# Two layers on one core: the order of the first loads and turns changed, and two orders of operations at the starts of two down projections

## The reference

```
h  = rmsnorm(x, norm_pre[0])                  # per position, over 2048 channels
z, xbc, dt = split(h @ ssd_w_in)              # 8 groups: 64 heads of 64, state of 128
xs, B, C = split(silu(causal_dwconv(xbc, 4 taps)))
dt = softplus(dt + dt_bias); a = dt * -exp(a_log)
y  = (C B^T * decay) (xs dt) + states from the chunk before + xs * d_skip
x  = x + rmsnorm(rmsnorm(y * silu(z)) @ ssd_w_out)
h  = rmsnorm(x);  q = h @ xa_w_q;  k, v = rmsnorm(mem) @ xa_w_kv      # 4 heads of 128
x  = x + rmsnorm(softmax(q k^T / sqrt(128)) v @ xa_w_o)
x  = x + rmsnorm(conv_ffn(rmsnorm(x)))        # 2048 -> 2 x 5632 -> 2048
# second layer: sparse and forgetting attention, then another conv_ffn, then the final norm
```

## Time and profile before

| | |
|---|---|
| median of three runs | 2713.67 us (2711.70 to 2715.04) |
| the profiled execution | 2714.08 us, of which the span is 2712.5 us |
| PE busy | 2678.1 us, 99% of the span |
| DVE, ACT, POOL busy | 64%, 49%, 6% |
| DMA | 503.41 MB, mean 186 GB/s |
| chain that ended last | PE 95%, DVE 2%, ACT 1%, issue 1% |

### The profile page before, as it was taken

The page is one execution under the profiler, slowest core; times in us unless marked ns, Lnnn a source line. Parts: engine busy times, 40 slices in busy tenths (PEclk is TensorE's granted clock), DMA queues, the critical chain, the costliest instruction groups (busy, mean ns, idle before and its releaser), DMA issues.

```text
span 2712.5 us, 37724 instructions
## 1 busy us (share of the span) xinstructions
PE 2678.1 (99%) x13921; PEld 2278.6 (84%) x13921; DVE 1736.5 (64%) x2133; ACT 1337.3 (49%) x1659; POOL 155.2 (6%) x130
## 2 busy tenths in 40 slices
PE   7999999999999999999999999999999999999998
PEld 6888888888778888888888887888888888888887
DVE  6777777754666767666744475644576766676444
ACT  5555555533566554555544464443465455545433
POOL 2311111100000000000000010000000000000000
PEclk9999999999999999999999999999999999999999
DMA  7555555565453555555555565434555555555552
GB/s 236 179 179 187 184 171 187 199 244 190 155 200 126 205 197 186 186 190 193 195 200 197 186 215 187 140 128 164 189 186 190 186 199 187 197 186 204 199 187 107
DMA packets 223163, 503.41 MB, mean 186 GB/s; under 512 B 15374, under 2 KB 50474, under 8 KB 202992
## 3 DMA queue, kind: packets, MB, share of 16 engines
q1 hardware_dynamic: 218160, 476.81, 52.2%
q0 software_dynamic: 4464, 24.99, 2.6%
q10 hardware_dynamic: 464, 0.59, 0.1%
HBM read 498.07 MB, written 4.28 MB: 185 GB/s over the span
## 4 chain that ended last, share of the span: by engine, by line
PE 95%; DVE 2%; issue 1%; ACT 1%; DMA 0%; SPq 0%; DVEq 0%; POOLq 0%; POOL 0%; ACTq 0%
PE PB L1214 14%; PE T L1214 13%; PE T L1522 12%; PE PB L1522 11%; PE PB L1168 9%; PE PB L1170 9%; PE PB L1169 9%; PE T L1525 6%; PE PB L1525 6%; PE T L1400 1%; PE T L1324 1%; DVE hT L1781 1%; DVE w_lo L1752 1%; PE T L1456 0%; DMA x<-in_x_dram 0%
## 5 line engine op out<-in xcount | busy, mean ns | idle before, releaser
L1752 DVE TENSOR_TENSOR w_lo<-raw,w_hi 128x2048 fp32r<-128x2048 f32 (+3 forms) x468 | 1037.6, 2224 | 598.4 <-ACT w_hi L714 596.5
L714 ACT ACTIVATE w_hi<-raw 128x2048 fp32r<-128x2048 f32 (+3 forms) x468 | 868.8, 1859 | 894.4 <-PE T L1214 384.6
L1168 PE MATMUL PB<-w_hi,hT 128*128 128x512 f32 (+3 forms) x1280 | 485.3, 379 | 5.4 <-DVE hT L1781 3.4
L1522 PE MATMUL T<-hT,w_hi 128*128 128x512 f32 x1408 | 489.7, 391 | 0.0
L1170 PE MATMUL PB<-w_hi,hT 128*128 128x512 f32 (+3 forms) x1280 | 471.3, 368 | 0.0
L1169 PE MATMUL PB<-w_lo,hT 128*128 128x512 f32 (+3 forms) x1280 | 471.1, 368 | 0.0
L1522 PE MATMUL PB<-hT,w_hi 128*128 128x512 f32 x1280 | 444.6, 391 | 0.0
L1525 PE MATMUL T<-hT,w_lo 128*128 128x256 f32 x1408 | 394.3, 280 | 0.0
L1525 PE MATMUL PB<-hT,w_lo 128*128 128x256 f32 x1280 | 358.4, 280 | 0.0
L1522 PEld LDWEIGHTS T<-hT,w_hi 128*128 128x128 f32 x1408 | 263.4, 187 | 58.0
L1214 PE MATMUL PB<-w_hi,hT 128*128 128x512 f32 x1120 | 305.2, 392 | 6.6 <-issue 3.0
(11 more groups left out here) (286 smaller groups left out, 2036.8 us busy)
## 6 DMA issues: line engine op xcount, KB each, us to landing
raw<-in_ffn_w_up_dram SPq DMA_DIRECT2D x88, 1024.0 KB, 5.1
raw<-in_w_up_dram SPq DMA_DIRECT2D x88, 1024.0 KB, 5.0
raw<-in_ssd_w_in_dram SPq DMA_DIRECT2D x64, 1024.0 KB, 5.2
raw<-in_ffn_w_down_dram SPq DMA_DIRECT2D x44, 1024.0 KB, 4.8
raw<-in_w_down_dram SPq DMA_DIRECT2D x44, 1024.0 KB, 4.8
raw<-in_w_in_dram SPq DMA_DIRECT2D x40, 1024.0 KB, 5.1
raw<-in_ssd_w_out_dram SPq DMA_DIRECT2D x32, 1024.0 KB, 4.8
raw<-in_ssd_w_in_dram SPq DMA_DIRECT2D x64, 256.0 KB, 3.2
```

The costliest lines, as they stand in the source:

```text
L714: nc.scalar.activation(dst, src, ACT.Copy).then_inc(hi_ready, 1)
L1168: nc.tensor.matmul(o, h, wh[:, c, :], start=(j == first and c == 0), stop=False)
L1522: ins = nc.tensor.matmul(banks[f][:, :], wh[:, c, s], both, start=(k == 0), stop=False)
L1752: V.tensor_tensor(dst, src, h.bitcast(F32), ALU.subtract).then_inc(lo_ready, 1)
```

## The change

It has three parts.

**Entry.** SP issues quad j of BCD ahead of block j of x (L549, then L555 in the changed file). ACT and DVE split quad j before they work on block j. PE turns block 0 before the first product, and block j + 1 inside quad j, after the first of its four chunks. Only the first 64 rows of parameters (`FIRST_ROWS`: the gains of three norms and of `norm_mem`) are loaded at once, by ACT's queue; POOL waits for block 2 of x before it issues the three broadcasts and the other 1008 rows, and PE turns those rows after quad 0 of unit 1 rather than before it. DVE copies them out two quads later than before. PE gets 14 small matmuls on the identity (`warm`), 4 before the first rows, 6 behind them, 4 behind block 0. ACT gets one tiny copy of 128x1 before its loop. The softplus scratch moves, since the rows lie longer in their place.

**`wout`.** In the last group, ACT and DVE make `down_first` right behind quad 0 of `wout` rather than after the convolution of xs, and DVE multiplies in the decays (L1977, `decayed`) behind quad 3 rather than before it.

**`xo`.** ACT splits chunks 0 and 1 before the high part of quad 3 rather than after; DVE copies out all four heads and splits chunks 0 and 1 before the low part of quad 3.

```diff
 NROWT = -(-NCOL // P)
+FIRST_ROWS = 4 * KC
...
-T_PLAN = [("params0", (0, 0, 1, 0)), (N_X, (2,) * 4), ("params", (1, 1, 0, 0)),
+T_PLAN = [("params0", (0, 0, 1, 0)), (N_X, (2,) * 4), ("params", (1, 1, 1, 0)),
...
         acsT = misc[0:HEADS, :]
-        sp_tmp = [big[:, 4096 + 128 * k:4096 + 128 * (k + 1)] for k in range(8)]
+        sp_tmp = [big[:, 5376 + 128 * k:5376 + 128 * (k + 1)] for k in range(8)]
...
             for name, a0, r, k in ROW_LOADS:
-                if (r < P) == first_tile:
+                if (r < FIRST_ROWS) == first_tile:
...
             for j in range(4):
+                load_bcd(j)
...
                     sp.dma_start(xt[:, tt, at], I["x"][0, tt * P:(tt + 1) * P, at]).then_inc(x_landed[j], 16)
-                load_bcd(j)
...
+            pool.wait_ge(x_landed[2], 32)
...
-            def down_first(name, ready):
+            def down_first(name, ready, js=range(4)):
...
                 act.wait_ge(quad_used, 4 * unit - 3)
-                for j in range(4):
+                for j in js:
...
             load_rows(act, True)
-            act.wait_ge(cols_ready, 1)
+            act.wait_ge(pool_own, 2)
+            nc.scalar.activation(mx[:, 0:1], ones[:, 0:1], ACT.Copy)
             for j in range(4):
+                hi_bcd(j)
+                if j == 0:
+                    act.wait_ge(cols_ready, 1)
...
                     h_hi(N_X, tt, "norm_pre", 0, None, (j,))
-                hi_bcd(j)
...
                 hi_next(0)
+                if not nxt:
+                    down_first("wout", lambda j: act.wait_ge(te[3], tb[3] + 2))
...
                 nc.scalar.activation(big[:, 9216:10240], big[:, 9216:10240], ACT.Silu).then_inc(xc_ready, 1)
-                if not nxt:
-                    down_first("wout", lambda j: act.wait_ge(te[3], tb[3] + 2))
...
                 prob_out(h)
-            hi_unit(U_XO, js=(3,))
-            down_first("xo", lambda h: xa_taken(act, h, (4, 4, 2, 2)[h]))
+            for js in ((0, 1), (2, 3)):
+                down_first("xo", lambda h: xa_taken(act, h, (4, 4, 2, 2)[h]), js)
+                if js == (0, 1):
+                    hi_unit(U_XO, js=(3,))
...
-            def up(q, pair, n, evac_before, after=None, norm=None):
+            def up(q, pair, n, evac_before, after=None, norm=None, inside={}):
...
                         if c in between:
-                            norm_transposes(norm[0], norm[1], 1, (between[c],))
+                            between[c]()
...
                         products(j, (0,), FIRST_TILE_ORDER[0], FIRST_TILE_ORDER[3],
-                                 {1: 0, 2: 1} if j == FIRST_TILE_ORDER[3] else {})
+                                 {1 + b: lambda b=b: norm_transposes(norm[0], norm[1], 1, (b,)) for b in range(2)}
+                                 if j == FIRST_TILE_ORDER[3] else {})
...
                         pe.wait_ge(lo_ready, q + j + 1)
-                    ins = products(j, (1,) if by_tile else (0, 1))
+                    ins = products(j, (1,) if by_tile else (0, 1), between=inside.get(j, {}))
...
-            pe.wait_ge(rows0_landed, 16 * sum(r < P for _, _, r, _ in ROW_LOADS))
-            turn_rows(0, 2, 0).then_inc(tf[2], 1)
...
+            def warm(n):
...
+                for _ in range(n):
+                    nc.tensor.matmul(T[3][:, 0:P], ident[:, :], ident[:, :], start=True, stop=True)
...
+            warm(4)
+            pe.wait_ge(rows0_landed, 16 * sum(r < FIRST_ROWS for _, _, r, _ in ROW_LOADS))
+            nc.tensor.transpose(T[2][:, 0:FIRST_ROWS], rows[0:FIRST_ROWS, 0, :], ident[0:FIRST_ROWS, 0:FIRST_ROWS]).then_inc(tf[2], 1)
+            warm(6)
             def turn_other_rows():
-                pe.wait_ge(rows_landed, 16 * sum(r >= P for _, _, r, _ in ROW_LOADS))
+                pe.wait_ge(rows_landed, 16 * sum(r >= FIRST_ROWS for _, _, r, _ in ROW_LOADS))
+                bank_free(2, TB["params"][2])
+                turn_rows(0, 2, 0).then_inc(tf[2], 1)
...
                     turn_group(N_X, 0)
-                    turn_group(N_X, 1)
-                    up(q, pair[0], BCD, None, {0: lambda: turn_group(N_X, 2), 1: lambda: turn_group(N_X, 3), 3: turn_other_rows}, (N_X, None))
+                    warm(4)
+                    up(q, pair[0], BCD, None, None, (N_X, None), {j: {0: lambda b=j + 1: turn_group(N_X, b)} for j in range(3)})
                 up(q + 4, pair[1], BLK, g * 3 + (E_SSD - 1) if prev else None,
-                   {2: lambda: (cumulative_sums(), turn_bc(g))} if not prev else
+                   {0: turn_other_rows, 2: lambda: (cumulative_sums(), turn_bc(g))} if not prev else
...
             dve.wait_ge(tf[2], 1)
-            V.tensor_copy(cols[:, 0:P], T[2][:, 0:P]).then_inc(te[2], 1)
+            V.tensor_copy(cols[:, 0:FIRST_ROWS], T[2][:, 0:FIRST_ROWS]).then_inc(te[2], 1)
...
             for j in range(4):
+                lo_unit(U_SSD, BCD, (j,))
...
                     h_lo(N_X, tt, "norm_pre", 0, (j,))
-                lo_unit(U_SSD, BCD, (j,))
             def other_cols():
+                dve.wait_ge(tf[2], TB["params"][2] + 1)
+                V.tensor_copy(cols[:, FIRST_ROWS:P], T[2][:, FIRST_ROWS:P]).then_inc(te[2], 1)
...
                             means(N_X, D)
-                            other_cols()
...
                             time_steps()
+                        if j == 2:
+                            other_cols()
...
                 lo_next(0)
+                if not nxt:
+                    down_first("wout")
...
                 lo_next(2)
-                if not nxt:
-                    down_first("wout")
-                decayed(g)
-                lo_next(3)
+                if nxt:
+                    decayed(g)
+                    lo_next(3)
+                else:
+                    lo_next(3)
+                    decayed(g)
...
                 lo_unit(U_XO, js=(1 + k,))
-            lo_unit(U_XO, js=(3,))
...
             xa_out(3)
+            lo_unit(U_XO, js=(3,))
```

## The result

The changed kernel takes 2706.49 us (median of 8 runs, 2705.59 to 2707.99) against 2714.24 us (8 runs) for the kernel before beside it: 7.8 us less, a ratio of 0.9972 (95% interval 0.9963 to 0.9981). Predicted were 2705.9 us and 7.8 us less. The profiled execution took 2706.38 us, its span went from 2712.5 to 2704.7. The total is right, but not every term: the entry gave 2.4 for 1.7, `wout` 1.2 for 1.45, `xo` 4.6 for 4.6, and 0.35 was lost between them.

The account below looks back on a forecast made before the run. PE, busy 99% of the span, was taken as the bound, so time comes off only where it waits or runs slowly. 1.7 (entry) + 1.45 (`wout`) + 4.6 (`xo`) = 7.8 us less, 2705.9 us predicted, range 2703.5 to 2708.

Parts of the forecast that it names:

- Step 1: Entry: with POOL's loads later, x's block 0 lands at 8.0 us (bounds 6.5, 11.2), block 1 at 12 to 13.
- Rival A: Entry: bound by the transfers; block 0 lands at 11.2, ACT is 1.3 us later; 2709.0 us, chance 0.13.
- Step 2: Entry: low part ready 4.5 us after turning a block, first products at 12.7 us against 15.80.
- Step 3: Entry: `warm` is worth nothing, PE's full clock comes at 17.1 us, quad 0 is done by 19.2.
- rival C: Entry: `warm` keeps PE at work, 2.4 GHz from first products, x sooner; 2 us more, 2703.7 us, chance 0.08.
- Steps 4 and 5: Entry: PE waits 0.5 us twice, ACT starts unit 1's quad 0 at 27.6, 1.7 us gained; quad lands at 27.2.
- Step 6: Entry's end: PE waits about 1.8 us at unit 1's quad 2; parameter rows there by 35, due at 37.9.
- Rival D: Unit 1: parameter rows come late and PE waits; slower than before, 2717 us with a late block 2, chance 0.05.
- The sum: Whole kernel: entry 1.7, `wout` 1.45 and `xo` 4.6 give 7.8 us off 2714.1; 2705.9 us predicted, chance 0.64.

Follow-up runs that it names:

- run 2: The changed kernel, but POOL does not wait for block 2 of x before its loads; 2713.00 us.
- run 1: The changed kernel without its 14 `warm` matmuls; 2708.22 us.
- run 6: The changed kernel with DVE multiplying in the decays before the low part of quad 3 again, only `down_first` staying moved; 2708.79 us.
- run 4: The changed kernel with its `xo` part undone and ten small matmuls put in PE's gap there; 2710.15 us.
- run 5: The changed kernel with its `xo` part undone and nothing put in the gap; 2711.94 us.
- run 10: The changed kernel with `wout` and `xo` as before, so the entry's part alone; 2712.95 us.
- run 12: The changed kernel with `wout` and `xo` as before, and ten small matmuls in PE's gap at `xo`; 2711.39 us.
- run 11: The kernel before, with ten small matmuls put in PE's gap at `xo`; 2712.60 us.
- run 9: The changed kernel with x's blocks turned earlier, one square before unit 1's quad 0, and the last group's `decays` behind ACT's taps; 2700.98 us.
- run 8: The changed kernel with x's blocks turned earlier and, in the last group, ACT's `decays` behind its taps and silu behind quad 3; 2703.50 us.

## Why the prediction was right

**Step 1 (when x lands): right, its size too small.** Block 0 came 0.6 us later than forecast (8.6 for 8.0). Of POOL's 4.7 us of engine time I had credited 3.2; run 2 shows that those loads cost x's block 0 5.0 us in this order. The upper bound I took for no effect, 11.2, was too low: with POOL's loads at once block 0 is turned at 13.6. Rival A is refuted: block 0 was turned at 8.59, and with the engines not freed 0.9 of the 7.8 us were left.

**Step 2:** first product 13.24 for 12.7. The way from turning to the low part took the 4.5 us forecast.

**Step 3 failed: "I give `warm` nothing".** It took the 9 transposes before as proof that small matmuls don't help, but idle of 3.9 us lay behind them. It also gave the 14 matmuls 3.2 us at most, the price of as many transposes; each is two records, and they took 6.1 (2.08, 2.93 and 1.10). Once begun they leave no idle above 1.8 us, PE is at full clock from 10.35, and run 1 shows 1.4 us. This is rival C's mechanism; it came at 1.4 instead of 2.

**Steps 4 and 5:** two waits of 0.5 each were forecast for block turning; there are three of 0.4 (0.56 by the starts: 17.56 to 18.27, where 0.15 is the pace). Unit 1's quad 0 came at 25.4 (27.2 forecast), so the landing was never the bound. ACT started at 26.89 for 27.6 forecast, and the step's logic is confirmed: PE's gain at 45.66 (2.39) is ACT's gain at 26.89 (2.40). But 27.6 was forecast without a gain from `warm`; without `warm`, in run 1, ACT started at 28.33. The path as forecast was 0.7 us worse than the sum had it, and 0.5 of that is block 0's delay (turned at 8.74 there, 8.2 forecast). **Step 6:** the wait before quad 2 was 1.4 for 1.8, and none was for the rows (PE turned them at 37.38). Rival D did not come: POOL issued its 19 loads (not 20) from 16.39 to 26.63, 0.54 us each as before, with DVE at work.

**`wout`:** the three waits were forecast at 0.3, 1.6 and 1.2 us, and came at 0.4, 1.4 and 1.0. (The "four more tiles" of 2.7 us behind tile 3 are two; the time is right.) The gain is 1.3 by the states and 1.2 by the turning of y behind them (556.60 for 560.16, less the entry's 2.39), for 1.45. That the clock would hold over these waits was right, and run 6 shows the other side: a wait of 2.9 us there brings it down.

**`xo`:** 4.57 for 4.6; runs 4 and 5 split it into the stall, 2.96, and 1.5 to 1.6 us of clock.

**The sum** came out at 2.39 + 1.17 + 4.57 = 8.1, less 0.35 that went between 557 and 802 (PE's waits for `hT` there are four of 1.5 us together, for three of 1.2): 7.8 in the trace, as forecast. Runs 10 and 12 have the same four waits, so it does not come from the orders at `wout` and `xo`. That the sum fits so closely is luck. Too little was forecast for `warm` (1.45); too much for the rest of the entry (0.76) and for `wout` (0.3), and the 0.35 were not in it at all.

## What to carry to other kernels

A long stall of PE can be paid twice: in its own length and in the clock behind it. The stalls of 2.9 us here were; waits of 1.0 to 1.8 us were not. A few small matmuls on data at hand, put so that no long idle is left before real work, save the second part; the order of the other engines saves both. When a wait is removed, follow the engine that produces the next operand: moving `down_first` alone only moved the stall three tiles on. And at a kernel's start keep small loads from another queue out of the way of the one block that everything waits for.

## What the runs showed of the hardware

The price of the same stall isn't fixed. From `xo`'s first product to ACT's first evacuation behind it are 8.04 to 8.06 us when the clock stays up (the changed kernel, runs 4, 11 and 12). Behind an idle of 2.90 or 2.91 us they are 9.66 in the kernel before, 9.57 with `xo` undone and 10.78 with the entry alone: the clock cost 1.6, 1.5 and 2.7 us. The PEclk of the windows gives more for the last, 4 x (0.30 + 0.50 + 0.05) = 3.4, but part of that fell before 809.52, while PE still stood idle. What made it longer there is not shown.

Run to run, times spread by 4.9 us where both stalls stand (run 10), by 1.8 in the kernel before with one gap filled, by 2.4 in the changed kernel and by 0.9 in run 9 (five runs). But run 8, with no such stall, spreads by 3.9 in five runs, so that the spread comes from the stalls is not shown.

The DMA share hides what small loads cost. With POOL's 19 loads under way, 0.62 MB in all, the engines looked 89% busy and moved 119 GB/s; with SP's loads alone 302 GB/s. By queue, in run 2 between 6 and 10 us (q1 has SP's loads, q0 POOL's; packets, MB, share of 16 engines):

```profile
q1 hardware_dynamic: 370, 0.40, 47.6%
q0 software_dynamic: 66, 0.07, 41.2%
```

POOL's 66 packets took nearly as much of the engines' time as SP's 370. The Trainium skill says that the engines take packets in turn from the queues that have work (DMA: Bandwidth & Descriptors, Queues, rings and completion order). These rows agree in so far as SP's loads got only about half of the engines' time while small packets were queued beside it; that the packets alternate, the rows don't show.
